# Attention's row factors: one 128x8 turning per tile, a trip through memory, and the scaling six units later

## The reference

```
z = rmsnorm(x) @ w_in                     # q, k, v of both mixers, gates
NSA:  o = g0*attend(q, compressed keys) + g1*attend(q, selected blocks) + g2*attend(q, window of 512)
DSA:  o = attend(q, top 256 keys by an indexer's score)
attend: p = exp(s - max s);  o = (p @ v) / sum(p)       # 8 heads of 64 channels each
h = x + (sigmoid(gA) * (o_nsa @ w_branch_nsa) + sigmoid(gB) * (o_dsa @ w_branch_dsa)) @ w_out
out = rmsnorm(h + SwiGLU(rmsnorm(h)))
```

## Time and profile before

| | |
|---|---|
| median of 3 runs | 1625.13 us (1624.43 to 1630.24) |
| profiled execution | 1625.18 us, span from first to last instruction 1623.2 us |
| TensorE | 1575.6 us busy (97%), 9008 matmuls |
| VectorE, ScalarE, GpSimd | 1157.2 us (71%), 651.4 us (40%), 639.8 us (39%) |
| granted TensorE clock, mean | 0.993 of full speed |
| attention's units | from about 424 to 789 us |

### The profile page before, as it was taken

One profiled execution on the slowest core, in us unless ns is written; L12 is line 12 of the kernel. 1 busy time (PEld: TensorE's weight loads), 2 busy tenths in 40 slices (PEclk: granted clock), 3 DMA queues, 4 the chain that ended last, 5 costly groups with the idle time before them and its releaser, 6 DMA issues.

```text
span 1623.2 us, 24586 instructions
## 1 busy us (share of the span) xinstructions
PE 1575.6 (97%) x9008; PEld 1328.0 (82%) x9008; DVE 1157.2 (71%) x2021; ACT 651.4 (40%) x1269; POOL 639.8 (39%) x442
## 2 busy tenths in 40 slices
PE   6999999999999989999999999999999999999997
PEld 5898888888798878898888887888888888877885
DVE  5745889999556667777665166667777766778978
ACT  5543322121566667767321144222222222343445
POOL 4234654221340144433221217444454545345454
PEclk9999999999999999999999999999999999999999
DMA  6033546331516010010255332333333334574433
GB/s 227 16 93 70 126 115 164 105 95 55 150 54 130 27 40 28 14 40 28 78 169 157 99 135 65 97 98 98 98 98 98 114 107 156 190 244 152 149 116 123
DMA packets 173303, 171.10 MB, mean 105 GB/s; under 512 B 25856, under 2 KB 126208, under 8 KB 173184
## 3 DMA queue, kind: packets, MB, share of 16 engines
q1 hardware_dynamic: 173184, 169.53, 34.5%
HBM read 122.04 MB, written 47.45 MB: 104 GB/s over the span
## 4 chain that ended last, share of the span: by engine, by line
PE 51%; DMA 5%; DVE 2%; POOL 1%; issue 1%; SPq 1%; ACT 0%; DVEq 0%; ACTq 0%
PE psA L1658 9%; PE psA L1659 9%; PE psA L1660 9%; PE psT L1660 5%; PE psT L1658 5%; PE psT L1659 5%; DMA wd<-in_w_down_dram 4%; PE psT L1665 3%; PE psT L1879 3%; PE psA L1768 1%; PE psA L1769 1%; DMA scratch_h<-h 0%; DMA s<-scratch_gates 0%; DVE h L2486 0%; DVE merged L2414 0%
## 5 line engine op out<-in xcount | busy, mean ns | idle before, releaser
L447 POOL TENSOR_TENSOR w_lo<-w_raw,w_hi 128x1024 fp32r<-128x1024 f32 (+2 forms) x52 | 119.9, 2307 | 256.6 <-ACT w_hi L442 256.3
L1257 POOL TENSOR_TENSOR w_lo<-w_sum,w_hi 128x1024 fp32r<-128x1024 f32 x44 | 115.4, 2628 | 119.5 <-ACT w_hi L1543 119.5
L1480 ACT ACTIVATE s<-s,nmax 128x640 f32<-128x640 f32 (+7 forms) x192 | 144.2, 753 | 29.5 <-DVE nmax L2356 27.9
L1281 POOL TENSOR_TENSOR w_lo<-act_raw,w_hi 128x512 fp32r<-128x512 f32 x77 | 109.7, 1426 | 106.9 <-ACT w_hi L1571 106.9
L1665 PE MATMUL psT<-ident,s 128*128 128x128 f32 x816 | 120.8, 278 | 0.8 <-ACT s L1480 0.8
L2577 DVE TENSOR_TENSOR w_lo<-wd,w_hi 128x512 fp32r<-128x512 f32 x77 | 94.9, 1235 | 23.5 <-ACT w_hi L1578 23.0
L442 ACT CAST w_hi<-w_raw 128x1024 fp32r<-128x1024 f32 (+2 forms) x52 | 52.7, 1018 | 141.5 <-PE psA L1660 81.1
L1665 PEld LDWEIGHTS psT<-ident,s 128*128 128x128 f32 x816 | 94.3, 141 | 17.2 <-issue 7.9
L2446 DVE COPY pT<-psT 128x512 f32<-128x512 f32 (+1 forms) x116 | 69.7, 601 | 53.7 <-PE psT L1665 53.5
L1571 ACT CAST w_hi<-act_raw 128x512 fp32r<-128x512 f32 x77 | 48.1, 625 | 127.5 <-PE psA L1660 59.5
L2246 DVE TENSOR_SCALAR_CACHE_REDUCE equal<-score,bit_try 128x512 f32<-128x512 f32 (+2 forms) x93 | 93.8, 1009 | 0.0
(11 more groups left out here) (380 smaller groups left out, 4675.0 us busy)
## 6 DMA issues: line engine op xcount, KB each, us to landing
act_raw<-scratch_act SPq DMA_DIRECT2D x77, 256.0 KB, 3.1
w_raw<-in_w_in_dram SPq DMA_DIRECT2D x24, 512.0 KB, 4.1
scratch_act<-act SPq DMA_DIRECT2D x33, 256.0 KB, 2.1
scratch_act<-act_sum SPq DMA_DIRECT2D x33, 256.0 KB, 2.1
wd<-in_w_down_dram SPq DMA_DIRECT2D x33, 256.0 KB, 3.1
scratch_gates<-gate_out SPq DMA_DIRECT2D x32, 256.0 KB, 3.1
gates<-scratch_gates SPq DMA_DIRECT2D x30, 256.0 KB, 4.1
a<-in_w_gate_dram SPq DMA_DIRECT2D x22, 256.0 KB, 3.3
```

The lines of the kernel that those rows point to most:

```text
L447: nc.gpsimd.tensor_tensor(lo, raw, hi.bitcast(F32), ALU.subtract).then_inc(self.lo_done, 1)
L1257: nc.gpsimd.tensor_tensor(lo2[n % RING][:], block_of(n)[:], hi2[n % RING][:].bitcast(F32), ALU.subtract)\
L1281: nc.gpsimd.tensor_tensor(lo2[slot][:, 0:512], act_raw[n % 6][:], hi2[slot][:, 0:512].bitcast(F32), ALU.subtract)\
L1480: a_.activation(s_sb[v % SR][:, 0:n], s_sb[v % SR][:, 0:n], ACT.Exp, scale=-1.0, bias=nmax[:, BR[a], i, h:h + 1], accum_out=psum_p[:, BR[a ...
```

## The change

The widening on GpSimd and the four turnings on TensorE go. Instead:

- VectorE makes the 128x8 factors at unit e+2 as before, now times the gate (a second operation of 128x8 in the NSA half).
- TensorE turns them at e+4, once, into 8x128.
- ScalarE copies this to `row_factors_turned` at e+5.
- SyncE stores it to memory (`scratch_factors`, 8 rows of 512 B), waits until the store has landed, and reads it back with two DMAs, each of which spreads four of the rows over 64 partitions (`row_factors_even` or `_odd`, 128x512). This is `turn_factors`.
- VectorE scales at e+13 instead of e+7, from this buffer instead of PSUM. What follows (`Y_LAG`) moves by six units too.

```
-    R_LAG = 3
-    O_LAG, F_LAG, Y_LAG = T_LAG + 1 + V_LAG + 1, T_LAG + 1 + V_LAG + 2, 8
+    R_LAG = 4
+    O_LAG, F_LAG, Y_LAG = T_LAG + 1 + V_LAG + 1, T_LAG + 1 + V_LAG + 2 + 6, 8 + 6
...
+        def turn_factors(t):
+
+            a, i = tiles6[t]
+            sp.wait_ge(t_act, act_took["r", a, i])
+            sp.dma_start(rD[t], factors_T[:]).then_inc(spilled[t % 2], 16)
+            if t >= 2:
+                sp.wait_ge(scaled_done, t - 1)
+            sp.wait_ge(*factors_spilled(t))
+            for r in range(2):
+                sp.dma_start(factors[t % 2][HD * r:HD * (r + 1)], rD[t:t + 1, r::2, :].to_broadcast([HD, 4, P]))\
+                    .then_inc(spilled[t % 2], 16)
+
         for k in range(2, 2 * NT):
+            if k >= NT + 2:
+                turn_factors(NT + 2 * (k - NT - 2))
             load_q(k)
+            turn_factors(k - 2 if k < NT + 2 else NT + 2 * (k - NT - 2) + 1)
...
+        for t in range(len(tiles6) - 4, len(tiles6) - 2):
+            turn_factors(t)
...
         load_gates(0)
         load_gates(1)
+        for t in range(len(tiles6) - 2, len(tiles6)):
+            turn_factors(t)
...
-            if tile_of(u, R_LAG):
-                a, i = tile_of(u, R_LAG)
...
-                pool.wait_ge(rows_done, t + 1)
...
-                    nc.gpsimd.tensor_tensor(r_wide[:], r, gate, ALU.mult).then_inc(wide_done, 1)
...
+            if tile_of(u - 1, R_LAG):
+                a, i = tile_of(u - 1, R_LAG)
+                act.wait_ge(t_ps, g6["r", a, i] + 1)
+                if t6[a, i]:
+                    act.wait_ge(*factors_spilled(t6[a, i] - 1))
+                a_.copy(factors_T[:], psT[0:H, g6["r", a, i] % 3, 0:P]).then_inc(t_act, 1)
...
-            if tile_of(u, O_LAG):
-                a, i = tile_of(u, O_LAG)
-                pe.wait_ge(wide_done, t6[a, i] + 1)
-                turn4(group(("r", a, i)), [r_wide[:, 2 * n:2 * n + 2, :].rearrange("p a d -> p (a d)") for n in range(4)])\
-                    .then_inc(t_ps, 1)
+            if tile_of(u, R_LAG):
+                a, i = tile_of(u, R_LAG)
+                pe.wait_ge(rows_done, t6[a, i] + 1)
+                pe.transpose(group(("r", a, i))[0:H, 0:P], psum_r[:, BR[a], i, :], ident[:]).then_inc(t_ps, 1)
...
+                then(v_.reciprocal(r, psum_p[:, BR[a], i, :]))
+                v_.tensor_tensor(r, r, nsa_gate[:, i, H * branch:H * (branch + 1)], ALU.mult).then_inc(rows_done, 1)
```

More of the change, by code:

```diff
@@ L203, in hybrid_block @@
     above, equal, nth_eq, below = (sb(work, f"blk_{n}", [P, KV, NSLC]) for n in ("above", "equal", "nth_equal", "below"))
-    sb(work, "skip_blk", [P, KV * NSLC * NSLC - KV * (TOPN + 1 + 4 * NSLC)])
+    sb(work, "skip_blk", [P, KV * NSLC * NSLC - KV * (TOPN + 1 + 4 * NSLC) - P])
     ya = [sb(work, f"ya{n}", [P, H * HD]) for n in range(2)]
@@ L207, in hybrid_block @@
     yt = sb(work, "ytmp", [P, H * HD])
-    r_wide = sb(work, "row_factors_wide", [P, H, HD])
+    factors_odd = sb(work, "row_factors_odd", [P, 4, P])
     c_st = sb(work, "c_st", [P, 4, H])
+    factors_T = sb(work, "row_factors_turned", [H, P])
     pg = sb(work, "p_group", [P, KV, 68])
@@ L219, in hybrid_block @@
     psum_r = sb(work, "psum_r", [P, 3, NT, H])
-    sb(work, "skip_merged", [P, HALF + 2 * HALF])
+    factors_even = sb(work, "row_factors_even", [P, 4, P])
+    sb(work, "skip_merged", [P, 2 * HALF])
     c_s = sb(work, "c_s", [P, H, 64])
@@ L606, in by_act @@
     def by_act(key):
-        return key[0] in ("ch", "cp") or (key[0] == "p" and key[1] % 2 == 0)
+        return key[0] in ("ch", "cp", "r") or (key[0] == "p" and key[1] % 2 == 0)
     act_took = nth([k for k in groups6 if by_act(k)])
     dve_took = nth([k for k in groups6 if not by_act(k)])
-    tiles6 = [k[1:] for k in groups6 if k[0] == "r"]
     t6 = {k: n for n, k in enumerate(tiles6)}
@@ L618, in y_ready @@
         if a == "dsa":
-            eng.wait_ge(t_dve, dve_took["r", a, i])
+            eng.wait_ge(scaled_done, t6[a, i] + 1)
         else:
@@ L650, in hybrid_block @@
     zt_ps, zt_out = sem("zt_ps"), sem("zt_out")
-    spilled = [sem(f"spilled{n}") for n in range(2)]
+    spilled = [sem(f"spilled_or_read_back{n}") for n in range(2)]
     id_ps, relu_done, sc_done = sem("id_ps"), sem("relu"), sem("score_sum")
@@ L667, in hybrid_block @@
     y_done, yh_done = sem("y_added"), sem("yh")
-    rows_done, wide_done = sem("row_factors"), sem("row_factors_wide")
+    rows_done, scaled_done = sem("row_factors"), sem("values_scaled")
     yl_done, yc_lo = sem("yl"), sem("y_chunk_lo")
@@ L698, in hybrid_block, with factors_spilled, factors_back @@
     kD = {"slc": scratch["k_slc"], "win": scratch["k_win"]}
-    gD = scratch["gates"]
+    gD, rD = scratch["gates"], scratch["factors"]
+    factors = [factors_even, factors_odd]
+    def factors_spilled(t):
+        return spilled[t % 2], spill_count(NT + 4 + t % 2) + 48 * (t // 2) + 16
+    def factors_back(t):
+        return spilled[t % 2], spill_count(NT + 4 + t % 2) + 48 * (t // 2 + 1)
     hD, aD = scratch["h"], scratch["act"]
@@ L1193, in _ @@
                 n, r = X_AT.index(u) // 2, X_AT.index(u) % 2
-                lows, wides = sum(1 for v in range(u) if y_of(v - 1)), sum(1 for v in range(u) if tile_of(v, R_LAG))
+                lows = sum(1 for v in range(u) if y_of(v - 1))
                 if lows:
                     pool.wait_ge(yl_done, lows)
-                if wides:
-                    pool.wait_ge(wide_done, wides)
                 windows(nc.gpsimd, n, r, (cx_k, cx_v)[n])
@@ L2375, in scaled @@
                     dve.wait_ge(y_done, n)
[L2376 removed]
+                v_.tensor_tensor(yt[:], wide, acc[t % 2][:], ALU.mult).then_inc(scaled_done, 1)
             elif i < HT:
                 y_free(dve, a, i)
[L2379 removed]
+                v_.tensor_tensor(y_of_tile(a, i)[:], wide, acc[t % 2][:], ALU.mult).then_inc(scaled_done, 1)
             else:
[L2381 removed]
+                v_.tensor_tensor(y_late("dsa", i), heads(wide, 4), heads(acc[t % 2][:], 4), ALU.mult).then_inc(scaled_done, 1)
         def cmp_out(i):
```

36 lines of the change are left out of this document (15 added, 21 removed).

## The result

The changed kernel takes 1641.56 us (median of 4 runs, 1640.38 to 1644.21) against 1624.78 us of the kernel before beside it; the ratio is 1.0105 with a 95% interval of 1.0086 to 1.0124. It is slower by about 17 us, where 18.6 were forecast. The span of the profiled execution is 1638.7 us (before 1623.2), its mean granted clock 0.987 (before 0.993).

What follows compares the result with a forecast made beforehand. TensorE was taken as the bound in attention's later part, with SyncE's queue deciding: -7.4 turnings, -3.0 widening, +9.2 first two places, +12.6 third, +3.3 clock, +3.9 tail = +18.6, so 1643.8 us; range 1631 to 1653.

Steps and rivals of the forecast that it cites:

- What decides: SyncE's DMA queue: it waits for the new store ahead of loads of q, compression weights and kT, deciding the sum.
- First and second place: SyncE's trips of tiles 0 and 1 delay weights and q of tiles 3 and 4; TensorE loses 9.2 us.
- the second place: Tile 1's store, queued behind q of tile 3, makes q of tile 4 land at 463.3; 3.8 us more lost.
- a rival price of 4.5 us less: At unit 32: if the queue kept no order, tile 1's store would take 2.1 us, not 6.6; no chance given.
- Third place with the clock: Tile 5's trip before kT delays q(8): TensorE loses 12.6 us, plus 3.3 for a half-clock stretch.
- Turnings: On TensorE, one turning instead of four saves 0.31 us a tile, 7.4 us over 24 tiles.
- The widening's waits: TensorE's 3.0 us of waits for `row_factors_wide` go; the new turning waits only for VectorE's 128x8 work.
- The tail: Last tile: `ytmp` starts 3.9 us late behind VectorE's four subtractions, delaying the product at 806.70.
- The rival on the other side: SyncE's waits are all hidden: 1618.7 us, or 1614.8 with the tail hidden too; chance 0.08.
- The one of a single place that bites: In SyncE's queue q of tiles 3 and 4 come nearly in time, 9.2 shrinks to about 1: 1635.6; chance 0.08.
- The slow read-back: Each read-back pair takes 10 us instead of 3.5, early places, third and tail grow by 6 each: 1668; chance 0.07.
- The turning that isn't cheaper: On TensorE, the turning with 8 columns costs as much as the four: 7.4 us more, 1651.2; chance 0.02.

Runs made afterwards that it cites:

- e2: Changed kernel without store and read-back, the factor buffers filled once with a constant; 1624.5 us, ratio 1.0003 to the kernel before.
- e7: Changed kernel with the two compression weights issued with q of tiles 4 and 5 instead of 2 and 3; 1635.0 us, ratio 1.0061.
- e5: Changed kernel with the 16 kT loads issued ahead of the store and read-back of tile 5; 1636.8 us, ratio 1.0064.
- e4: Changed kernel with the turned factors in the free half of the accumulator's bank, copied one unit later; 1644.5 us, ratio 1.0116.
- e1: The kernel before, unedited, profiled for one more execution; span 1618.7 us against 1623.2 in its first profile.
- e10: The kernel before with only the two compression weights issued with q of tiles 4 and 5; 1623.1 us, ratio 0.9998.
- e12: Changed kernel without store and read-back (constant factors), turned factors in the accumulator's bank, VectorE's four subtractions behind the last scaling; 1615.9 us, ratio 0.9953.
- e6: Changed kernel with VectorE's four low-part subtractions of y_dsa put behind the last tile's scaling; 1641.0 us.
- e3: Changed kernel with store and read-backs issued from ScalarE instead of SyncE; 1629.2 us, ratio 1.0029.
- e8: Changed kernel with trip issued from ScalarE, factors in accumulator's bank, subtractions behind last scaling, weights with q of tiles 4 and 5; 1632.2 us, ratio 1.0044.

## Why the prediction held, point by point

- **What decides.** That the sum is decided on SyncE was right: without the trip the loss is gone (e2). 17.1 us are the trip's.
- **First and second place.** Forecast 9.2 us, shown 7.4 (after against e2), and with the weights moved away none of it is left (e7). But the 7.4 are not the two waits of the forecast. At unit 24 TensorE waits 5.71 us, near the 5.4 of the forecast, though it also got there 2.6 us earlier than before, so that the product itself is only 2.85 us late. At unit 32 the forecast has 3.8 us more, and the trace a wait of 0.72: the second place is no loss to speak of, since q of tile 4 is there at 460.2 and not at 463.3. What fills the gap is 2.6 us of low clock behind the first wait, which the prediction had only in its upper bound. The sum of this term is near by luck.
- **SyncE's times there.** The weights of k went out at 435.41, forecast 436.2, since ScalarE's copy was 1.6 us earlier than taken from the earlier trace rows; the store took 2.9 us, forecast 2.5 from the earlier trace rows. The second store came back in 6.3 us, forecast 6.6. That it lies behind q was the step with a rival price of 4.5 us less; e5's 13.9 us behind kT settles it.
- **Third place with the clock.** Forecast 12.6 + 3.3 = 15.9 us, shown 14.4 in the trace (13.1 against e2). This place is right in mechanism and in size. q(8) landed 25.3 us after the first kT issue, forecast 25.4 from the earlier trace rows; TensorE's wait was 14.5, forecast 14.7. The store was quicker than taken (1.3 instead of 2.5 us). The low clock lay for the greater part in the wait itself: of 17.0 us TensorE worked 5.18, of which half, 2.6, is the loss. With the 2.6 behind unit 24 the new stretches cost more than the 3.3 that the sum has for the clock. The old stretch of the earlier trace rows, which the prediction thought might go with the widening, is still there.
- **Turnings.** Right in TensorE's work, 0.33 us a tile against 0.31, though both of its terms were off. The earlier trace rows is the last tile; ahead of a product of scores four turnings took 0.36 us and not 0.41 (731.15 to 731.51 in the trace before). The timeline of e4 shows one new turning: 0.03 us to the next product, below both nearest rows, and the earlier trace rows, and not 0.10.

```profile
728.97 0.27 PE L1958 MATMUL psT<-ident,psum_r 128*8 128x128 f32 x1
729.00 0.36 PE L1788 MATMUL psA<-kT_win,q 128*128 128x256 f32 x1
```

- **The widening's waits.** This step failed. It said that the new turning waits only for VectorE's 128x8 work, and gave 3.0 us to the gain. The turning had been moved to unit e+4, behind that unit's transposes, where its psT bank is still being emptied; it waits 4.9 us there, and the other waits grew by about 1 us. Idle time grew by 3.4 us in 112 units where 3.0 should have gone. Turnings and waits together gave about 1.2 us in that window, not the greater part of 10.4. With a bank of its own it was 3.8 (197.00 against 193.20).
- **The tail.** Forecast 3.9 us from VectorE's order at the product of 806.70. That product stands at 826.43, 19.7 us later, of which 18.0 were there at 775: 1.7 us, not 3.9. `ytmp` is 2.9 us late, the load of w_raw behind it 2.4 (818.07 against 797.67), and the gates' load is 0.7 quicker than before (4.61 against 5.28). The other 1.6 of the 3.3 that the table shows by 820 are a low-clock stretch of 3.4 us behind this product. Every kernel here with the subtractions in front or the trip in place has such a stretch; before, e1, e10 and e12 have none. Without the trip the tail costs 4.0 (e2); 2.5 is VectorE's order (e12).
- **The sum.** 18.6 us were forecast and 16.8 measured, but two errors cancel, which is luck: the gain was some 6 us too large (no-trip kernel: forecast 1618.7, measured 1624.5), and the trip was put at 25.1 us where it costs 17.1. In the trace the three places are 4.6 us cheaper than forecast (20.5 in all against 25.1); the other 3.4 us can't be settled from medians and single profiles: at 820 us the trip is still worth 20.5 us (21.3 against 0.8), at 1500 it is 17.6 (15.5 against -2.1), and the stage between differs by several us in e1 without an edit.
- **The rival on the other side**, all waits on SyncE hidden, was given 1618.7 and 1614.8. The kernels without the trip reach 1620.9 and, with the tail in order, 1615.9, but only with the bank wait taken away as well.
- **The other rivals.** The one of a single place that bites comes half true: the second place doesn't, but the first does. The slow read-back is out: in e6 the pair issued at 803.73 was there at 808.24, and in after VectorE waits for no read-back at all. The turning that isn't cheaper is out by the 0.33 us. (The high ends of the terms add up to 33.6 and not to 32; no chance rests on it.)

## What to carry to other kernels

Before a round trip through memory is put on an in-order queue, list what stands behind it and look at what lies ahead on the same DMA engines: in these kernels a 4 KB store cost the bytes ahead of it, whichever engine issued it, and whoever waited for it stood that long. A wait that is taken away has to be followed to the buffer that the new instruction needs, not only to its data; here a third of the forecast gain went into the rotation of three banks. A forecast that hits the total can have wrong terms that cancel: take out one part alone (no trip) before believing it, and look within each place at what is wait and what is low clock.

## What the runs showed of the hardware

- A store of 4 KB was back in 1.3 us in an empty queue (after, tile 5), 2.9 us with the end of one q ahead (tile 0), 6.3 us behind a whole q (512 KB) and the rest of the weights of k (tile 1), and 13.9 us behind what was left of 4 MB (e5).
- Another engine's queue hardly passes such bytes. With kT ahead, the store of tile 5 was back 23.0 us after the first kT issue on SyncE's queue (e5, 506.96 to 529.93), and on ScalarE's it was 20.7 in e3 (502.76 to 523.44) and 22.6 in e8 (500.26 to 522.87). A read-back of 256 KB issued from ScalarE at 434.27, beside q of tile 3 and the weights on SyncE's queue, was there at 444.4. The Trainium skill ("DMA: Bandwidth & Descriptors", Queues, rings and completion order) says that descriptors are taken in ring order, that each issuing engine has a ring of its own, and that a DMA engine takes the rings that have work in turn. By ring order the store behind kT should be late, and e5 shows it. By turns a short transfer on an idle ring should not wait for all that the other ring holds; e3's 10 us and its store's 4.9 us (429.40 to 434.27) are longer than that suggests. The same section also says that a DMA's semaphore increment lands only after every earlier write of that DMA engine, across its queues, and so a short store may be told late; no run here took these shares apart.
- A turning with 8 stationary columns takes 0.03 us to the next product (e4, 728.97 to 729.00), where one with 128 takes 0.09 (before, four from 731.15 to 731.51). The weight load's own record is still 87 ns long (median in e4). By the Trainium skill ("TensorE: Matmul & The Clock Gate", LDWEIGHTS) the load would be some 7 ns, and the estimate made of it was 56 ns a turning; the total saved was close (0.35 forecast by the page, 0.33 shown).
